# Two transformer blocks with routed experts on one core: the branch around the overflow rounds turned over, a closing pair of 64 and 64 slots, and another order in the first body of both expert stages

## What is computed

```python
combine = sum_k one_hot(global_idx[k]) * weights[k]      # two experts per token, in one group
for e in range(N_EXPERTS):
    h = silu(x @ w_gate[e]) * (x @ w_up[e])
    y = y + combine[:, e:e+1] * (h @ w_down[e])
```

## Time and profile before

| | us |
|---|---|
| median of 3 runs | 1435.55 |
| lowest, highest | 1434.66, 1435.93 |
| the profiled execution | 1433.75 |
| its span | 1432.0 |
| PE, DVE, ACT, POOL busy | 1309.0, 504.9, 366.3, 307.8 |

### The profile page before, as it was taken

The page is one execution under the profiler, slowest core; times in us unless marked ns, Lnnn a source line. Parts: engine busy times, 40 slices in busy tenths (PEclk is TensorE's granted clock), DMA queues, the critical chain, the costliest instruction groups (busy, mean ns, idle before and its releaser), DMA issues. The chain is left out here.

```text
span 1432.0 us, 26492 instructions
## 1 busy us (share of the span) xinstructions
PE 1309.0 (91%) x11524; PEld 851.9 (59%) x11524; DVE 504.9 (35%) x935; ACT 366.3 (26%) x680; POOL 307.8 (21%) x350
## 2 busy tenths in 40 slices
PE   7999989888899999998969999998899899989994
PEld 6778754577645654454448878896545554444432
DVE  6278335432334321111173157653522501001016
ACT  2323147344222111111142242233522211111112
POOL 8354212254000200000023422450000211111100
PEclk9999999999999999999989999999999899999997
DMA  6812000300073799999951111103052589999983
GB/s 222 300 59 82 37 1 0 120 4 4 4 269 118 281 416 416 416 417 418 412 192 60 59 60 59 60 1 118 1 188 94 208 344 357 412 411 416 404 349 145
DMA packets 75339, 284.03 MB, mean 198 GB/s; under 512 B 14966, under 2 KB 16317, under 8 KB 62930
## 3 DMA queue, kind: packets, MB, share of 16 engines
q1 hardware_dynamic: 68592, 267.47, 47.8%
q0 software_dynamic: 5056, 10.56, 2.0%
q10 hardware_dynamic: 1570, 4.24, 0.8%
HBM read 258.62 MB, written 29.06 MB: 201 GB/s over the span
## 5 line engine op out<-in xcount | busy, mean ns | idle before, releaser
L390 POOL TENSOR_TENSOR arena_mix<-ring 128x512 f32<-128x512 f32 x52 | 69.3, 1351 | 170.6 <-PE banks L425 124.8
L1705 PE MATMUL banks<-ring,mixT 128*128 128x512 f32 x224 | 99.1, 595 | 3.9 <-PEq L50 3.2
L435 ACT ACTIVATE arena_mix<-banks 128x256 f32<-128x256 f32 x104 | 39.4, 382 | 234.5 <-PE banks L425 234.5
L2059 POOL DMA_INDIRECT expert_rows<-arena_moe x21 | 20.5, 974 | 366.1 <-ACT arena_moe L2386 183.8
L425 PE MATMUL banks<-ring 128*128 128x256 f32 x416 | 96.2, 380 | 1.6 <-DVE arena_mix L446 1.0
L2101 DVE TENSOR_TENSOR mixT<-banks,params 128x512 f32<-128x512 f32 (+2 forms) x64 | 38.1, 596 | 140.5 <-PE banks L2076 83.2
L446 DVE SCALAR_TENSOR_TENSOR arena_mix<-banks,arena_mix 128x256 f32<-128x256 f32 x78 | 32.0, 422 | 156.8 <-ACT arena_mix L435 89.0
L425 PEld LDWEIGHTS banks<-ring 128*128 128x128 f32 x416 | 78.3, 190 | 14.0 <-issue 3.6
L2076 PE MATMUL banks<-G_moe,x_hi_moe 128*128 128x256 f32 (+2 forms) x320 | 82.0, 295 | 4.5 <-issue 4.5
L2076 PE MATMUL banks<-G_moe,x_lo_moe 128*128 128x256 f32 (+2 forms) x320 | 80.3, 290 | 0.0
L425 PE MATMUL banks<-ring,arena_mix 128*128 128x256 f32 x320 | 72.4, 380 | 0.7 <-ACT arena_mix L435 0.7
(11 more groups left out here) (511 smaller groups left out, 2554.0 us busy)
## 6 DMA issues: line engine op xcount, KB each, us to landing
ring<-in_w_in SPq DMA_DIRECT2D x26, 1024.0 KB, 7.5
arena_moe<-in_exp_w_gate SPq DMA_DIRECT2D x16, 1024.0 KB, 12.4
arena_moe<-in_exp_w_up SPq DMA_DIRECT2D x16, 1024.0 KB, 16.4
arena_moe<-in_exp_w_down SPq DMA_DIRECT2D x16, 1024.0 KB, 16.0
ring<-in_exp_w_gate SPq DMA_DIRECT2D x16, 1024.0 KB, 12.8
ring<-in_exp_w_up SPq DMA_DIRECT2D x16, 1024.0 KB, 15.5
ring<-in_exp_w_down SPq DMA_DIRECT2D x16, 1024.0 KB, 17.6
arena_moe<-in_w_gate SPq DMA_DIRECT2D x8, 2048.0 KB
```

What stands on the lines that cost most here:

```text
L390: pool.tensor_tensor(out[:, c], a[:, c], b[:, c], op).then_inc(ph.sem("weight_sums"), 1)
L435: act.activation(self.dest(n, i)[block], self.m.banks[a][:, 0:256], ACT.Copy, scale=self.scale(n)).then_inc(ph.sem(name), 1)
L1705: last = pe.matmul(m.banks[k % 3][:], m.mixT[:, c, i * P:(i + 1) * P], w[:, c, :], start=(c == 0), stop=(c == DC - 1), skip_group_check=True)
L2059: pool.indirect_dma_start(z.d.outputs, bass.IndirectOffsetOnAxis(ap=place[:, c:c + 1].bitcast(U32), axis=0), z.y[:, 2 * c:2 * c + 2, :].re ...
```

## The change

It has four parts.

1. The branch (`run_ahead`, for PE and DVE only). `If(n < 1)` now holds the first body itself (PE: the first gathering and body 0; DVE: the four `turned_rows_dve` of body 0 and then `entries`), and `Else` holds the overflow rounds and a second copy of the first body. With zero rounds nothing is jumped over at the test, and there is a jump over the other arm at the end of the first body.
2. `entries` moves on DVE from ahead of body 0's gathered rows to behind them; `split` of the last rows stays ahead.
3. The first body. In block 1 the gate products of a unit run ahead of its up products and signal apart (`gates`), the down parts run ahead of the second gathering, and SP loads the gates of body 1 at `gates`. In block 2 `down_first` runs ahead of the up products of unit 2 and of the gathering, `down_second` ahead of the second gathering, and SP's order for body 1 follows that.
4. The last body of block 2 holds the two experts with the fewest tokens in 64 slots each: two units of 64-row products instead of two and a rest, one output tile pair instead of three pieces, `one_sums_pe` with 16 products instead of 16 and 32 smaller ones, the low parts on DVE between the additions, and `load_outputs` one unit earlier. `order_experts` gets two small operations more, `load_main_slots` two loads more. More than 6 experts (before: 7) of the 14 above 64 tokens now call for an overflow round.

```diff
-        return self.slots if body == 0 or not self.wide else self.cap + 64
+        if body == 0 or not self.wide:
+            return self.slots
+        return P if body == self.bodies - 1 else self.cap + 64
...
+    def last_split(dve):
+        split(dve, NT - 1)
...
-    first = z.bodies
+    first = z.bodies - 1
     v.link(dve.scalar_tensor_tensor(z.keys, z.totals, float(E), z.tie, ALU.mult, ALU.add))
     v.link(dve.tensor_tensor(z.pairs[:, 2:, 1:], z.keys[:, 1:].unsqueeze(1).broadcast_to([P, E - 2, E - 1]),
                              z.keys[:, 2:].unsqueeze(2).broadcast_to([P, E - 2, E - 1]), ALU.is_gt))
     v.link(dve.tensor_reduce(z.greater[:, 2:], z.pairs[:, 2:, 1:], AX_X, ALU.add))
-    v.link(dve.tensor_scalar(z.keys[:, 2:], z.greater[:, 2:], float(first), float(3 - E), ALU.is_ge, ALU.mult))
+    v.mark(dve.tensor_scalar(z.later[:, 2:], z.greater[:, 2:], float(E - 2), -3.0, ALU.is_ge, ALU.mult))
+    v.link(dve.tensor_scalar(z.keys[:, 2:], z.greater[:, 2:], float(first), float(5 - E), ALU.is_ge, ALU.mult))
+    v.link(dve.tensor_tensor(z.keys[:, 2:], z.keys[:, 2:], z.later[:, 2:], ALU.add))
...
+    def run_ahead(self, engine, begin, body, end, ahead, none, behind):
+        n = self.rounds_of(engine)
+        with engine.If(n < 1):
+            none()
+        with engine.Else():
+            ahead()
+            self.repeat(engine, n, begin, body, end, False)
+            behind()
...
+def one_sums_pe(pe, ph, m, z):
+    def half(t, n):
         for part in (z.y_hi, z.y_lo):
-            for k in range(2):
-                g = (k + flip) % 2
-                for n in range(2):
-                    a = 64 * n + 32 * g
-                    last = pe.matmul(m.banks[2 * (t + k) + n][:, 256 * g:256 * g + 256], z.ST[a:a + 32, 1, (t + k) * P:(t + k + 1) * P],
-                                     part[a:a + 32, 2, 0:256], start=False, stop=(part is z.y_lo), skip_group_check=True)
-                    if part is z.y_lo:
-                        last.then_inc(ph.sem("quartered" if flip == 0 else "quarters"), 1)
-    pe.wait_ge(ph.sem("quarters"), 2 * t + 4)
-    pe.sem_inc(ph.sem("summed"), 2)
+            last = pe.matmul(m.banks[2 * t + n][:], z.ST[:, 0, t * P:(t + 1) * P], part[:, n, :], start=(part is z.y_hi),
+                             stop=(part is z.y_lo))
+        if n == 1:
+            last.then_inc(ph.sem("summed"), 1)
+    pe.wait_ge(ph.sem("chosen_slots"), 1)
+    pe.wait_ge(ph.sem("y_low"), 1)
+    half(0, 0)
+    half(1, 0)
+    pe.wait_ge(ph.sem("y_low"), 2)
+    half(0, 1)
+    half(1, 1)
+    for t in range(2, NT):
+        half(t, 0)
+        half(t, 1)
...
-    sp.wait_ge(ph.sem("hidden"), z.units * (z.bodies - 1) + (2 if z.wide else 1))
+    sp.wait_ge(ph.sem("hidden"), z.units * (z.bodies - 1) + 1)
...
+                if i == 1 and s % 2 == 0:
+                    sp.wait_ge(ph.sem("gates"), s // 2 + 1)
+                    for k in range(2):
+                        z.load_in(sp, io, s + k, i, ring_sems[s + k], (0,))
+                    sp.wait_ge(ph.sem("hidden"), s // 2 + 1)
+                    for k in range(2):
+                        z.load_in(sp, io, s + k, i, ring_sems[s + k], (1,))
+                elif i > 1:
+                    sp.wait_ge(ph.sem("hidden"), 2 * i + s // 2 - 1)
+                    z.load_in(sp, io, s, i, ring_sems[s])
...
+        def first_gates_before_ups(u):
+            slots = range(2 * u, 2 * u + 2)
+            for s in slots:
+                pe.wait_ge(ring_sems[s], 32)
+            for part in range(2):
+                for j in range(DC):
+                    if u == 0 and part == 0 and j % 2 == 0:
+                        pe.wait_ge(ph.sem("gathered_taken"), j // 2 + 1)
+                    for k, s in enumerate(slots):
+                        both, _ = z.slot(s)
+                        last = pe.matmul(hb[u][k * cap:(k + 1) * cap, 256 * part:256 * part + 256], z.xe[:, j, s * cap:(s + 1) * cap],
+                                         both[:, part, j, :], start=(j == 0), stop=(j == DC - 1), skip_group_check=True)
+                last.then_inc(ph.sem("gates" if part == 0 else "hidden"), 1)
...
+        def body_0():
+            first_gates_before_ups(0)
+            first_gates_before_ups(1)
+            turn_hidden(ph, 0, 0)
+            pe.wait_ge(ph.sem("onehot"), 2 * ONEHOTS)
+            gather_pe(pe, ph, z, gath, 0, None)
+            turn_hidden(ph, 0, 1)
+            down(ph, 0, 0, ring_sems)
+            down(ph, 0, 1, ring_sems)
+            gather_pe(pe, ph, z, gath, 1, 4)
...
+    further.run_ahead(pe, lambda r: None, body, end, lambda: None, first, first)
...
+    def rows_and_entries():
+        first()
+        entries(dve)
+    further.run_ahead(dve, begin, body, lambda n: dve.nop(), lambda: entries(dve), rows_and_entries, first)
...
+                z.load_in(sp, io, 1, 1, ring[1], (0,), e[1])
+                sp.wait_ge(ph.sem("down"), 2)
+                z.load_down(sp, io, 0, 1, ring[2], e[0])
+                sp.wait_ge(ph.sem("hidden"), 3)
+                z.load_in(sp, io, 1, 1, ring[1], (1,), e[1])
+                sp.wait_ge(ph.sem("down"), 3)
+                z.load_down(sp, io, 1, 1, ring[3], e[1])
+                continue
...
+        def last_gate_up(u):
+            pe.wait_ge(ring[u], 32 * NB)
+            both, _ = z.expert(u)
+            for j in range(DC):
+                if u == 0 and j % 2 == 0:
+                    pe.wait_ge(ph.sem("gathered_taken"), 4 * (NB - 1) + j // 2 + 1)
+                for half in range(2):
+                    last = pe.matmul(hb[u][64 * half:64 * half + 64, :], z.xe[:, j, 64 * u:64 * u + 64],
+                                     both[:, :, j, half * 256:half * 256 + 256], start=(j == 0), stop=(j == DC - 1),
+                                     skip_group_check=True)
+            last.then_inc(ph.sem("hidden"), 1)
+        def last_down():
+            pe.wait_ge(ph.sem("turned_hidden_taken"), 3 * (NB - 1) + 2)
+            for s in range(2):
+                pe.wait_ge(ring[2 + s], 16 * NB)
+            for n in range(2):
+                for h in range(2):
+                    for f in range(2):
+                        for s in range(2):
+                            _, wd = z.expert(s)
+                            last = pe.matmul(yb[n][64 * s:64 * s + 64, :], z.hT[:, s, f, 64 * h:64 * h + 64],
+                                             wd[:, 2 * h + f, n * HW:(n + 1) * HW], start=(h == 0 and f == 0),
+                                             stop=(h == 1 and f == 1), skip_group_check=True)
+                last.then_inc(ph.sem("down"), 1)
+        def last_body():
+            last_gate_up(0)
+            last_gate_up(1)
+            turn_hidden(ph, NB - 1, 0)
+            turn_hidden(ph, NB - 1, 1)
+            pe.wait_ge(ph.sem("y_taken"), 3 * (NB - 1))
+            last_down()
...
+        def body_0():
+            gate_up(ph, 0, 0, ring)
+            gates_before_ups(0, 1)
+            turn_hidden(ph, 0, 0)
+            gates_before_ups(0, 2, (0,))
+            turn_hidden(ph, 0, 1)
+            down_first(ph, 0, ring)
+            gates_before_ups(0, 2, (1,))
+            next_rows(1, 0, None)
+            turn_hidden(ph, 0, 2)
+            down_second(ph, 0)
+            next_rows(1, 1, 4)
...
         early(0)
+        y_low_dve(dve, ph, z, 0, yb[0], z.main.weight[:, NB - 1, 0:1])
         early(1)
-        rest_hidden(NB - 1)
+        y_low_dve(dve, ph, z, 1, yb[1], z.main.weight[:, NB - 1, 0:1])
         early(2)
         early(3)
-        for i in range(3):
-            y_low_dve(dve, ph, z, i, yb[i], z.main.weight[:, NB - 1, i // 2:i // 2 + 1], HW if i < 2 else 256)
```

More of the change, by code:

```diff
@@ L1631, in load_slots @@
         if self.wide:
-            part(0, 0, 0, 32, self.cap)
+            for first, last, rank in ((0, self.E - 2, 32), (self.E - 2, self.E - 1, 0)):
+                src = table[bass.ds(first_rank + rank, self.cap), first:last, :]
+                engine.dma_start(slots.rows[0:self.cap, 0, first:last, :], src).then_inc(sem, 16)
             part(self.cap, 0, 1, 64, self.cap - 64)
@@ L2089, in turn_rows_pe @@
             j = 4 * half + 2 * a + b
-            for c, count in enumerate((P, width - P)):
+            for c, count in enumerate((P, width - P) if width > P else (P,)):
                 at = b * width + c * P
@@ L2181, in chosen_slots_dve @@
 def chosen_slots_dve(dve, ph, z):
-    for c in range(2):
+    for c in range(1 if z.wide else 2):
         dve.tensor_scalar(z.ST[:, c, :], z.ramp, z.main.token[:, z.bodies - 1, c:c + 1], None, ALU.is_equal).then_inc(ph.sem("chosen_slots"), 1)
@@ L2451, in first_rows_pe, with further_pe @@
     gather_pe(pe, ph, z, second, 1, None)
[L2454 removed]
+def further_pe(pe, further, z, x, x_ring, body, first):
     def end(n):
@@ L2463, in end, with further_dve @@
         pe.sem_inc(x.sem("reloaded"), 1)
-    further.run(pe, lambda r: None, body, end)
-def further_dve(dve, further, z, x, rest):
```

(14 more changed lines are left out.)

147 lines of the change are left out of this document (60 added, 87 removed).

## The result

The changed kernel took 1449.02 us (median of 7 runs, 1444.66 to 1450.43), the kernel before beside it 1435.93; the ratio is 1.0079 [1.0052, 1.0106]. The profiled execution has a span of 1444.7 us, 12.7 more than the 1432.0 of before.

What follows compares the result with a forecast made beforehand. The prediction took memory traffic as the bound: a body costs its bytes. Block 1 +0.7, block 2's start +4.0 and its end -8.0 sum to -3.3 us, so 1435.55 becomes 1432.2 us, range 1425.5 to 1440.5.

Steps and rivals of the forecast that it cites:

- The tail: End of block 2, last weights' landing to first addition of sums: 25.2 us instead of 33.2, so -8.0 us.
- rival C: End of block 2: output loads late, DVE still waits for expert_rows, tail gives half; 1436.2 us, chance 0.13.
- rival A: Block 2's first gathering: PE keeps its clock, late table costs 1.2 us, not 4.0; 1429.4 us, chance 0.24.
- s: PE's stall at the jump ending body 0 in block 1: taken as 2.8 us, bounds 0 and 4.49.
- max(-0.7, s - 2.1): Block 1's cost from the earlier gate load, stream gap and stall s at PE's jump: +0.7 us.
- Rival B: PE's jump behind body 0: s = 9, block 1 costs 6.9 us, block 2 5.7; 1440.2 us, chance 0.20.
- the gap of 2.8 us: Block 1, body 1's weight stream: no bytes from 492.6 to 495.4, waiting for the late slot loads.
- distance of 12.15 us: End of entries to first slot load, taken from block 2 for block 1 too; gave 480.65 + 12.15.
- T: The experiments' theory of the late table, entries behind the gathered rows; the forecast's block 2 start had +4.0 us.
- body 2's first gate goes out at 1192.7: Block 2, start of the stream: 5.0 us later than before, after body 1's first weights at 1158.8.
- The late start: Block 2: body 1's first weights go out at 1158.8 instead of 1148.1, 10.7 us later.
- The sum: Whole kernel: 0.7 + 4.0 - 8.0 = -3.3 us, median 1435.55 becomes 1432.2; chance 0.40.

Runs made afterwards that it cites:

- e7: Changed kernel keeping only the closing pair; branch, place of entries and first bodies' order as in the kernel before: 1424.94 us, ratio 0.9952.
- e12: e7 again, on another chip: 1426.56 us, ratio 0.9956 to the kernel before.
- e3: Changed kernel with entries on DVE ahead of the test and gathered rows, as before; both branches stay turned: 1442.35 us, ratio 1.0076.
- e14: e3 again, beside e13 on one chip: 1444.08 us, ratio 1.0084 to the kernel before.
- e2: Changed kernel with the other arm of PE's branch a single no-operation (overflow rounds and second copy left out): 1439.70 us, ratio 1.0061.
- e1: Changed kernel with PE testing the rounds as in the kernel before, no jump behind body 0; entries stay late: 1441.98 us, ratio 1.0081.
- e5: The changed kernel again, unaltered, on another chip: 1442.96 us against 1432.66 of the kernel before, ratio 1.0069.
- e4: Changed kernel with branch and place of entries as before on PE and DVE; new body 0 order and closing pair stay: 1420.28 us, ratio 0.9924.
- e6: e4 with DVE's branch turned as in the changed kernel, entries ahead: 1423.43 us, ratio 0.9932 to the kernel before.
- e11: e4 again, on another chip: 1425.69 us, ratio 0.9951 to the kernel before.
- e9: Changed kernel with the other arm of PE's branch holding the overflow loops alone, without the second copy: 1439.59 us, ratio 1.0067.
- e13: e3 with the edit of e2 (PE's jump passes one instruction): 1425.97 us, ratio 0.9948 to the kernel before.

## Why the prediction was wrong

**The tail was right, partly by luck.** Forecast -8.0, with 25.2 us from landing to sums; 26.0 was measured, the two marks -7.2. Its terms were off and made up for each other: the unit's products took 7.1 us at a granted clock of 1.00 instead of 8.8, the down products 8.8 (clock 0.77 over their first 7.3 us) instead of 7.1. With what lies ahead of it in the last body, the rest of block 2 went from 227.8 to 219.4. The down weights, which cost up to 1.5 us, were not in the sum; DVE did wait 5.5 us for the output rows ahead of its first addition, but the second low part, behind which four additions stand, waited for ACT, so this was not rival C. The first gathering of block 2 ran at a granted clock of 0.50 in its first 3 us, so rival A did not come either. The closing pair by itself made 7.7 and 7.1 us in e7 and e12.

**Block 1: the step that failed is "I take 2.8" for s.** The cost of the jump was written as max(-0.7, s - 2.1). The two idle times are 8.8 us, with which the formula gives 6.7; the marks show 7.0 - 0.4 = 6.6. Rival B had s = 9 and 6.9: it named the right cause and size for this block. That the numbers agree so closely is luck: body 2's first weights went out 11.5 us later than before (525.41 against 513.89), not 8.8, since the unit behind the idle time also ran at a low clock at first (7.93 us from 517.01 on, before 7.03 for the whole unit), and the same idle with an early table came with 256.2 and 258.6 us (e3, e14), 8 to 11 more than before.
```
after            505.39  519.20  525.07  531.04  550.37
e2 (one passed)  504.64  527.38  548.31
```

At the jump the second and third come 5.9 us apart, one in each of the two idle times and 2.6 and 2.4 us ahead of its end, where without the long jump there is one in 20 us. Where the price begins, and why it is less with 452 instructions passed than with 298, was not found; that it depends on where the code lies is a guess.

**Block 1, the gap of 2.8 us was also too small**, only hidden by the jump: slot loads went out at 495.43, not 492.8. The distance of 12.15 us from entries to slots came from block 2, where no weights are under way; here POOL's last scatter is issued by 491.1 and has landed 4.3 us later, against 1.2 there. T alone costs this block some 5 us against the kernels with an early table.

**Block 2: "body 2's first gate goes out at 1192.7", 33.9 us after body 1's, failed.** The late start itself was right (first weights 48.5 behind the block's first load, forecast 1158.8 - 1109.1 = 49.7). But in e1 and e2 body 2's first gate follows 38.5 and 38.7 us after it. I let the last up weights land 29.1 us after the first weights; they took 32.3 in e2, where five of the six loads went out within 5 us and the sixth 11 us behind the first. That they then share the memory is not shown by itself, but down weights issued among them (1171.53) took 25.9 us to land. And I gave PE's unit 4.6 us until it releases SP, where it needs 6.3: it had been idle for 7 us and started at half its clock. So T costs 9 to 11 us there against the kernel before (87.6 and 89.8 in e2 and e1, 78.6 before), not 4.0. With this the jump (rival B: 1.7 more) adds little (87.1 in e5), though alone it costs 7.5, roughly (4 and 11). In the first profile after 42.5 us lie between the two first weights, since PE's pauses came on top; some 4 of the 12.5 us are theirs, and they were in nobody's sum.

**The sum**: 6.6 + 12.5 - 8.4, and 2 us between the marks (0.4 ahead of the experts, 1.7 between the blocks), are the 12.7 measured. Rival B had the sign and block 1; nothing had T's 9 to 11 us. Two small slips of the working change nothing: 513.9 + s + 1.4 against 517.5 is s - 2.2, and the upper bound of block 2 is 5.0 - 0.3 + 1.5 = 6.2 by its own terms. The chance of 0.23 for slower was too low, as the two costs were each bounded by rows of another situation.

## What to carry to other kernels

- A turned branch costs what its jump costs at the place where it then stands. At the test the wait lay beside other waiting; behind body 0 it stood ahead of the unit that releases the next weights. Count the instructions that are passed, and put a long jump where the engine waits anyway.
- Work that is only wanted "later" (the table for body 1) must be followed to the transfer that waits for it, and in a stage bound by memory on to the idle engine and its clock when the data comes at last.
- When undoing either of two suspects changes nothing, undo both before acquitting them: e1, e2 and e3 each looked like an acquittal, e4 showed over 19 us on that chip.

The version that beats both kernels is e4 (or e7, which differs from it by nothing measurable): 0.992 to 0.996 of the kernel before.

## Seen on the hardware and not expected

- Behind a taken jump TensorE idled not at all with 1 instruction passed, 3.9 us with some 106, 8.8 with 298 (in two pieces of 3.7 and 5.1 us) and 6.1 with 452. At the test ahead of the rows the same engine idled 4.49, 1.2, 1.4, 1.7 and 3.3 us in before, e1, e4, e6 and e7. The same code differs too: 1.5 us in e11, which is e4 again, and 2.0 in e12, which is e7 again.
- In the profile after, and in e9, PE issued its short products in unit 1 of block 2's body 0 with four pauses of up to 0.85 us, and the unit took over 15 us instead of 7.1. The same code in e5 had none. In e13 and e14 it had three and took 10.4 us. POOL was scattering the table just then in after, e9 and e5; the cause is open.
- The profiles' first mark of block 1 lies between 451.0 and 461.8 us, though nothing ahead of it was changed, and from block 1's first output load to block 2's first weights it is 406.3 to 416.0 us; profiles of single executions are better compared stage by stage than by their spans.
